# Experts' down product: both halves of the contraction as three fp32r products, and two more residual tiles parked in DRAM

## The reference

```python
def swiglu(h, w_gu, w_down):
    gate, up = jnp.split(h @ w_gu, 2, axis=-1)      # w_gu  1024 x 512
    return (jax.nn.silu(gate) * up) @ w_down        # w_down 256 x 1024

    def expert_block(acc, blk):
        tok, wts, e = blk
        out = swiglu(h_pad[tok], w_gu[e], w_down[e])
        return acc.at[tok].add(out * wts[:, None].astype(out.dtype)), None
```

## Time and profile before

| | us |
|---|---|
| median of 3 runs (2133.29 to 2133.43) | 2133.34 |
| profiled execution, its own time | 2129.38 |
| span of the profiled execution | 2127.6 |
| TensorE busy in the span | 2043.8 (96%) |
| VectorE busy | 1310.2 (62%) |
| ScalarE busy | 1008.7 (47%) |

### The profile page before, as it was taken

How to read it: one execution, slowest core, us unless ns; L and a number is a source line. 1 busy time by engine, 2 the same in 40 slices (tenths; PEclk the granted TensorE clock), 3 DMA queues, 4 the chain that set the end, 5 groups by cost and what they waited for, 6 DMA issues and landing times.

```text
span 2127.6 us, 33319 instructions
## 1 busy us (share of the span) xinstructions
PE 2043.8 (96%) x12264; PEld 1696.5 (80%) x12265; DVE 1310.2 (62%) x1968; ACT 1008.7 (47%) x1474; POOL 279.5 (13%) x217
## 2 busy tenths in 40 slices
PE   7999989999999999999999998999999999999998
PEld 3788977889767667777767767998978897898898
DVE  3868578445778668888868867357643444423433
ACT  4335455323467667777767754334332224312322
POOL 0004023000222332333333310000000000000000
PEclk9999999999999999999999999999999999999999
DMA  9831111262789879999979973211122223222221
GB/s 356 290 121 45 57 60 60 98 253 120 281 315 335 295 257 356 352 365 370 367 282 374 363 268 133 80 60 42 60 82 95 99 80 109 96 83 99 98 81 60
DMA packets 76953, 393.56 MB, mean 185 GB/s; under 512 B 16353, under 2 KB 32865, under 8 KB 46337
## 3 DMA queue, kind: packets, MB, share of 16 engines
q1 hardware_dynamic: 57794, 358.38, 44.8%
q0 software_dynamic: 19008, 33.22, 6.3%
HBM read 384.56 MB, written 43.01 MB: 201 GB/s over the span
## 4 chain that ended last, share of the span: by engine, by line
PE 61%; DMA 5%; DVE 4%; ACT 2%; issue 2%; DVEq 0%; SPq 0%; POOLq 0%; ACTq 0%
PE bank L3402 17%; PE bank L2306 4%; PE bank L2332 4%; PE bank L2310 4%; PE bank L2309 4%; DMA moe_work<-in_experts_dram 4%; PE bank L3085 3%; PE bank L3087 3%; PE bank L3086 3%; PE bank L3070 2%; PE bank L3072 2%; PE bank L3071 2%; PE bank L2292 2%; DVE moe_gu_rest L2067 1%; PE bank L2335 1%
## 5 line engine op out<-in xcount | busy, mean ns | idle before, releaser
L2687 DVE TENSOR_TENSOR b_w_rest<-ring,b_w_high 128x2048 fp32r<-128x2048 f32 x63 | 144.4, 2292 | 179.6 <-ACT b_w_high L2682 179.2
L2306 PE MATMUL bank<-moe_gu_high,moe_x_high 128*128 128x512 f32 x512 | 210.2, 411 | 17.0 <-DVE moe_gu_rest L2067 9.6
L2682 ACT ACTIVATE b_w_high<-ring 128x2048 fp32r<-128x2048 f32 x63 | 120.5, 1912 | 177.3 <-PE bank L3402 126.8
L2309 PE MATMUL bank<-moe_gu_rest,moe_x_high 128*128 128x512 f32 x512 | 202.5, 396 | 0.0
L2310 PE MATMUL bank<-moe_gu_high,moe_x_rest 128*128 128x512 f32 x512 | 202.5, 395 | 0.0
L3086 PE MATMUL bank<-b_w_rest,b_h_high 128*128 128x256 f32 x608 | 171.6, 282 | 0.0
L3085 PE MATMUL bank<-b_w_high,b_h_high 128*128 128x256 f32 x544 | 156.9, 288 | 2.8 <-DVE b_h_rest L2717 1.7
L2067 DVE TENSOR_TENSOR moe_gu_rest<-moe_work,moe_gu_high 128x2048 fp32r<-128x2048 f32 x64 | 146.3, 2286 | 18.0 <-ACT moe_gu_high L1804 17.8
L3087 PE MATMUL bank<-b_w_high,b_h_rest 128*128 128x256 f32 x544 | 153.9, 283 | 0.0
L2067 DVE TENSOR_TENSOR moe_gu_rest<-ring,moe_gu_high 128x2048 fp32r<-128x2048 f32 x64 | 146.3, 2287 | 11.1 <-ACT moe_gu_high L1804 11.1
L3402 PE MATMUL bank<-b_w_high,hidden_high 128*128 128x256 f32 x512 | 144.9, 283 | 0.0
(11 more groups left out here) (524 smaller groups left out, 5318.5 us busy)
## 6 DMA issues: line engine op xcount, KB each, us to landing
ring<-in_stream_dram SPq DMA_DIRECT2D x105, 1024.0 KB, 4.9
moe_work<-in_experts_dram SPq DMA_DIRECT2D x32, 2048.0 KB, 13.0
moe_work<-in_experts_dram SPq DMA_DIRECT2D x64, 1024.0 KB, 7.4
ring<-in_experts_dram SPq DMA_DIRECT2D x32, 2048.0 KB, 13.4
X<-in_stream_dram SPq DMA_DIRECT2D x16, 512.0 KB, 7.5
mixer_work<-in_stream_dram SPq DMA_DIRECT2D x16, 512.0 KB, 6.1
X<-in_x_dram SPq DMA_DIRECT2D x8, 512.0 KB, 8.7
ffn_sums<-mixer_work SPq DMA_DIRECT2D x8, 512.0 KB, 4.9
```

What stands on the lines that cost most here:

```text
L2306: first = mm(banks[2][:, :], xh[:, k, :], wh[h][:, c], start=(k == 0), stop=False)
L2309: mm(banks[2][:, :], xh[:, k, :], wl[h][:, c], start=False, stop=False)
L2682: nc.scalar.activation(high_at(u), raw(u), ACT.Copy).then_inc(s["w_high"], 1)
L2687: nc.vector.tensor_tensor(WL[u % FEED], raw(u), high_at(u), ALU.subtract).then_inc(s["w_rest"], 1)
```

## The change

Both halves of the down product become three fp32r products. For that ScalarE copies both halves of the down weights to `DH` (two passes of 1,024 columns per expert in place of one), VectorE subtracts twice (two passes in place of one), the transposed hidden activations are copied and subtracted as 256 columns at once (one ScalarE pass in place of two of 128), and TensorE issues six fp32r products per output half in place of one plain and three. The two more `DH` buffers lie in the tiles 1 and 2 of `X`, so these are stored to DRAM too: behind the rows of h2 of the same tile at the end of the stage before, and loaded back behind the experts. Some small buffers move. The diff, without the like edits for the further blocks:

```diff
@@ -176,7 +176,7 @@
             "xn": nc.dram_tensor("h2_rows", [TOK, D], F32),
             "rows": nc.dram_tensor("ada_rows", [1, 4 * D], F32),
             "sums": [nc.dram_tensor(f"ffn_sums{k}", [TOK, D], F32) for k in range(2)],
-            "last_rows": nc.dram_tensor("residual_last_tile", [P, D], F32),
+            "parked": nc.dram_tensor("residual_tiles", [NT * P, D], F32),
         }
 
         s_unit = [es.enter_context(nc.semaphore(f"unit_arrived{i}")) for i in range(RING)]
...
@@ -475,8 +475,10 @@
             for t in range(NT):
                 sp.wait_ge(s["h2_ready"], t + 1)
                 sp.dma_start(dram["xn"][t * P:(t + 1) * P, :], H2[:, t, :]).then_inc(s["h2_stored"], 16)
+                if t in (1, 2):
+                    sp.dma_start(dram["parked"][t * P:(t + 1) * P, :], X[:, t, :]).then_inc(s["h2_stored"], 16)
             sp.wait_ge(s["zero_stored"], 32 * NT)
-            sp.wait_ge(s["h2_stored"], 16 * NT)
+            sp.wait_ge(s["h2_stored"], 16 * (NT + 2))
 
         @block.gpsimd
         def _(pool):
...
@@ -1498,13 +1500,14 @@
     ONEHOT = [grid(mem["place"](f"onehot{k}", EXACT + 816 + 256 * k, 512, BF16)[:, :], 4) for k in range(2)]
     ONEHOTX = grid(mem["place"]("onehot_further", EXACT + 1328, 512, BF16)[:, :], 4)
     CNT = take(NE).bitcast(I32)
-    SG, HID, HDT = take(256), take(256), [take(P) for _ in range(2)]
+    SG, HID = take(256), take(256)
     HDT_AT = at[0]
-    take(256)
-    HDTH = [exact(f"hidden_high{k}", AT_WORK + HDT_AT + P * k, P) for k in range(2)]
-    HDTL = [exact(f"hidden_rest{k}", AT_WORK + WORK + P * k, P) for k in range(2)]
-    DH = [exact(f"down_high{k}", o, D) for k, o in enumerate((AT_X + (NT - 1) * D, EXACT + 1712))]
-    DL = [exact(f"down_rest{k}", AT_WORK + 2 * GU + DN * k + D, D) for k in range(2)]
+    take(512)
+    HDTH = [exact(f"hidden_high{k}", AT_WORK + HDT_AT + 256 * k, 256) for k in range(2)]
+    HDTL = [exact(f"hidden_rest{k}", AT_ADAROW + 512 + 256 * k, 256) for k in range(2)]
+    DH_AT = ((AT_X + D, AT_X + 3 * D), (AT_X + 2 * D, EXACT + 1712))
+    DH = [[exact(f"down_high{p}{k}", DH_AT[p][k], D) for k in range(2)] for p in range(2)]
+    DL = [[exact(f"down_rest{p}{k}", AT_WORK + 2 * GU + DN * p + D * k, D) for k in range(2)] for p in range(2)]
 
     TOKI, ROWI = take(4).bitcast(I32), take(4).bitcast(I32)
     TWA, TWX = take(136).rearrange("p (e c) -> p e c", c=2), [take(2) for _ in range(2)]
...
@@ -1690,12 +1693,15 @@
             sums_back(1)
             sp.wait_ge(s["dn_done"], NE - 1)
             sp.wait_ge(s["rows_moved"], 32)
-            sp.dma_start(X[:, NT - 1, :], dram["last_rows"][:, :]).then_inc(s["rows_moved"], 16)
+            sp.wait_ge(s["shared_down_in"], 16)
+            sp.dma_start(X[:, 1, :], dram["parked"][P:2 * P, :]).then_inc(s["shared_down_in"], 16)
             unit_in(0)
             sums_back(2)
             sums_back(3)
             unit_in(1)
+            sp.dma_start(X[:, 3, :], dram["parked"][3 * P:4 * P, :]).then_inc(s["rows_moved"], 16)
             sp.wait_ge(s["dn_done"], NE)
+            sp.dma_start(X[:, 2, :], dram["parked"][2 * P:3 * P, :]).then_inc(s["rows_moved"], 16)
             unit_in(2)
             unit_in(3)
             then["sync"](sp)
...
@@ -1836,15 +1842,16 @@
             def copy_hdt(i, o):
                 after(act, "ht2_done", i, o, 1)
                 after(act, "dn_done", i, o - 2, 1)
-                nc.scalar.activation(HDTH[o % 2], banks[3][:, P:2 * P], ACT.Copy).then_inc(s["down_highs"], 1)
-                nc.scalar.activation(HDT[o % 2], banks[3][:, 0:P], ACT.Copy).then_inc(s["down_highs"], 1)
+                nc.scalar.activation(HDTH[o % 2], banks[3][:, 0:2 * P], ACT.Copy).then_inc(s["down_highs"], 1)
 
             def dn_high(i, o):
                 act.wait_ge(s_dn[o % 2], 16 * (o // 2 + 1) + 32 * i)
                 after(act, "dn_done", i, o - 2, 1)
                 if isinstance(i, int) and 4 * i + o == 0:
                     act.wait_ge(s["rows_moved"], 32)
-                nc.scalar.activation(DH[o % 2], dnslot[o % 2][:, D:2 * D], ACT.Copy).then_inc(s["down_highs"], 1)
+                for k in range(2):
+                    nc.scalar.activation(DH[o % 2][k], dnslot[o % 2][:, D * k:D * (k + 1)], ACT.Copy).then_inc(
+                        s["down_highs"], 1)
 
             def further_split(n):
                 for h in range(2):
...
@@ -2069,13 +2075,15 @@
 
             def dn_rest(i, o):
 
-                after(dve, "down_highs", i, o, 1, 3)
-                v.tensor_tensor(DL[o % 2], dnslot[o % 2][:, D:2 * D], DH[o % 2], ALU.subtract).then_inc(s["down_rests"], 1)
+                for k in range(2):
+                    after(dve, "down_highs", i, o, 1 + k, 3)
+                    v.tensor_tensor(DL[o % 2][k], dnslot[o % 2][:, D * k:D * (k + 1)], DH[o % 2][k], ALU.subtract).then_inc(
+                        s["down_rests"], 1)
 
             def hdt_rest(i, o):
 
                 after(dve, "down_highs", i, o, 3, 3)
-                v.tensor_tensor(HDTL[o % 2], banks[3][:, P:2 * P], HDTH[o % 2], ALU.subtract).then_inc(s["down_rests"], 1)
+                v.tensor_tensor(HDTL[o % 2], banks[3][:, 0:2 * P], HDTH[o % 2], ALU.subtract).then_inc(s["down_rests"], 1)
 
             def x_rest(i, o):
 
...
@@ -2218,6 +2226,7 @@
             f_both(1)
             weighted(1)
             next_inverse(0)
+            dve.wait_ge(s["shared_down_in"], 32)
             mixed(1)
             sums_of_two(2)
             next_inverse(1)
...
@@ -2229,9 +2238,9 @@
             f_both(3)
             then["w_rest"](dve, 1)
             weighted(2)
+            dve.wait_ge(s["rows_moved"], 64)
             mixed(2)
             weighted(3)
-            dve.wait_ge(s["rows_moved"], 48)
             mixed(3)
             dve.wait_ge(s["f_tile"], 2 * NT)
             for t in (2, 3):
...
@@ -2313,29 +2322,26 @@
             def turn_hidden(i, o):
                 after(pe, "hid_ready", i, o, 1)
                 after(pe, "down_highs", i, o - 1, 3, 3)
-                after(pe, "down_rests", i, o - 1, 2, 2)
+                after(pe, "down_rests", i, o - 1, 3, 3)
                 for k in range(2):
                     last = nc.tensor.transpose(banks[3][:, k * P:(k + 1) * P], HID[:, k * P:(k + 1) * P], ident)
                 last.then_inc(s["ht2_done"], 1)
 
             def down_ready(i, o, bank=4):
                 after(pe, "down_highs", i, o, 3, 3)
-                after(pe, "down_rests", i, o, 2, 2)
+                after(pe, "down_rests", i, o, 3, 3)
                 if bank == 4:
                     after(pe, "out_act", i, o - 1, 2, 2)
-                pe.wait_ge(s_dn[o % 2], 16 * (o // 2 + 1) + 32 * i)
-
-            def down_products(bank, j, k, o, plain, high, rest):
-
-                c = slice(512 * j, 512 * (j + 1))
-                if k == 0:
-                    return mm(bank[:, :], plain, dnslot[o % 2][:, c], start=True, stop=False)
-                mm(bank[:, :], high, DH[o % 2][:, c], start=False, stop=False)
-                mm(bank[:, :], high, DL[o % 2][:, c], start=False, stop=False)
-                return mm(bank[:, :], rest, DH[o % 2][:, c], start=False, stop=True)
+
+            def down_products(bank, j, k, o, high, rest):
+
+                c, at = slice(512 * j, 512 * (j + 1)), slice(P * k, P * (k + 1))
+                mm(bank[:, :], high[:, at], DH[o % 2][k][:, c], start=(k == 0), stop=False)
+                mm(bank[:, :], high[:, at], DL[o % 2][k][:, c], start=False, stop=False)
+                return mm(bank[:, :], rest[:, at], DH[o % 2][k][:, c], start=False, stop=(k == 1))
 
             def down_part(i, o, j, k, bank=4):
-                product = down_products(banks[bank + j], j, k, o, HDT[o % 2], HDTH[o % 2], HDTL[o % 2])
+                product = down_products(banks[bank + j], j, k, o, HDTH[o % 2], HDTL[o % 2])
                 if (j, k) == (1, 1):
                     product.then_inc(s["dn_done"], 1)
 
...
```

24 lines of the change are left out of this document (11 added, 13 removed).

## The result

The changed kernel takes 2173.23 us (median of 4 runs, 2170.92 to 2175.27), the kernel before 2133.32 on the same chip (4 runs): a ratio of 1.0198, 95% interval 1.0185 to 1.0212. It is 2% slower. The profiled execution went from 2129.38 to 2175.27 us, its span from 2127.6 to 2173.5, +45.9; the sum of the prediction had said +41.7 between profiled executions.

A forecast was written before the change was run, and what follows sets the result against it. TensorE sets the calm pace, 9.94 us per expert; a silu-to-silu chain of 9.64 lies close, stretched to 10.78 by the pass. Ordinary experts +38.1, with special intervals and the end +41.7: 2133.34 + 41.7 = 2175, range 2163 to 2189.

The forecast's parts named there:

- The chain and its price: Silu to silu through VectorE's rests: the added pass makes ordinary experts 10.78 us each, +38.1 over 54.
- TensorE's saving is lost: Down product: 0.44 us saved per expert, spent waiting about 1.2 us before the second half.
- ScalarE's second pass costs nothing: Second dn_high copy ends 0.20 us before VectorE wants it: cost 0, at most 0.1 per expert if late.
- Late loads vanish: Down weights: ScalarE's 13.9 us of waits in 21 experts disappear as loads get more room.
- the lateness stays: Rival: down-weight loads stay as late relative to use, +13.9 on top, 2189 us; chance 0.10.
- The nine special intervals: Long silu intervals: two first-loop-pass, three second blocks, three searches, one scatter wait; +4.6 in sum.
- The two of the first loop pass: TensorE's first pass through its loop: two intervals with long waits and lower clock gain 0.44 each, -0.9.
- The searches: Three intervals searching for a second block, steps following w_rest in the chain: +1.13 each, +3.4.
- the second blocks: Three experts with a second block: pass adds 1.13, shorter down product saves 0.44; +0.7 each, +2.1.
- The end and the parking: Behind the experts -1.0, between -2 and +1; storing and reloading two more tiles 0.
- The clock rival: Waits of 1.2 us per expert lower TensorE's clock: +104 in every expert, +26 in every fourth, 2201; chance 0.07.
- The hidden pass: Rival: VectorE's extra pass costs the chain nothing, TensorE's saving counts, pace 9.64, time 2108; chance 0.05.

The follow-up runs named there:

- The single-pass experiment: Kernel before, with the parking and one more unused VectorE subtraction of 1,024 columns ahead of dn_rest: 2175.16 us, ratio 1.0215.
- the two-pass one: Kernel before, with the parking and two extra VectorE passes ahead of dn_rest, the second in all experts but the last: 2256.61 us, ratio 1.0601.
- the version without the second rest: Changed kernel without VectorE's subtraction for the down weights' second half, whose products take the first half's rest: 2123.85 us, ratio 0.9972.
- the version without the first rest: Changed kernel without VectorE's subtraction for the down weights' first half; all products take the second half's rest: 2163.84 us, ratio 1.016.
- all four versions: Changed kernel, second half's rest on GpSimd, behind or ahead of its gather, VectorE's rest in place or behind w_rest: 2175.79, 2201.48, 2314.88, 2191.78 us.
- the last version: Changed kernel, second half's rest on GpSimd ahead of its gather, VectorE's first-half rest behind the next expert's w_rest: 2191.78 us, ratio 1.0297.
- the early GpSimd pass: Changed kernel, second half's rest on GpSimd ahead of its gather, VectorE's first-half rest left in place: 2314.88 us, ratio 1.0865.
- e8: Changed kernel, second half's rest on GpSimd behind its gather, first half's on VectorE behind the next expert's w_rest: 2201.48 us, ratio 1.034.
- e1: Changed kernel with both VectorE dn_rest passes behind the next expert's w_rest, but ahead of any second block: 2148.27 us, ratio 1.008.
- e9: Kernel before with its one dn_rest moved behind the next expert's w_rest: 2129.57 us, ratio 1.0003.

## Why the prediction was right

Forecast 2175, measured 2173.2. By its steps:

- **The chain and its price.** Right. Predicted 10.78 per ordinary expert, 54 of them for +38.1; measured 584.2 us for the 54, +40.1. Of these, 51 lie between 10.71 and 10.92, 10.79 each; the rest are the first two (12.18, with a low clock, and 11.28) and one of 10.23 behind the scatter wait. The single-pass experiment shows that the pass alone makes this (584.0 us for the same 54), the two-pass one that the chain passes on each further 1.13, and the version without the second rest that the interval falls back to 9.6 where loads allow (10.04 on average).
- **TensorE's saving is lost.** Right: 12 products in some 2.85 us, and a wait of 0.96 (predicted about 1.0 as recorded).
- **ScalarE's second pass costs nothing.** Right, with 0.32 to spare where 0.20 was expected; the version without the first rest shows what it costs without that cover.
- **Late loads vanish.** Right: the wait of the earlier trace rows is gone from the larger ones, and the ordinary intervals hardly differ. So the rival "the lateness stays" (0.10) is out.
- **The nine special intervals.** Wrong in its terms, +7.1 against +4.6 in sum. The two of the first loop pass lost 6.2 us instead of 0.9: they are 11.16 and 10.82 now, since neither the long waits nor the low clock of the earlier trace rows are there; why the waits went is open. The searches gained 7.9 instead of 3.4, the second blocks 6.4 instead of 2.1. What was left out is that waits already there grow to about 2 us with the pass and can bring the low clock, at some 1.5 us each: three times in the searches, in two of the three second blocks. Without those five the searches come to +3.4 as predicted, and the second blocks to +3.4, three times the pass: the 0.44 that I credited to each for the shorter down product was not gained. The wait of 12.74 became 11.64, 1.1 less, where I had 0. The errors nearly cancel, which is luck.
- **The end and the parking.** -1.3 for everything outside the first to the last silu, against -1.0 predicted; parking 0, as measured by itself.
- **The clock rival** (0.07). It is excluded for the ordinary experts: 53 of the 54 intervals have a clock of 1.00, and the other is the stage's first, with its wait of 2.36. But it came true in five special intervals, which I had not priced. The 1.23 us at 578.12 spoke against it, and rightly for waits of that length; both low-clock intervals of the earlier trace rows hold a longer one, though, the 2.01 of the earlier trace rows and one of 2.60 at 608.03 that I had not used. That every expert has a wait does not by itself bring the fall (two extra passes, 1.7 to 1.8 us each).
- **The hidden pass** (0.05) is excluded by the experiment with one pass and nothing else.

The profiled execution says +45.9 and the medians say +39.9: the one of before lies 4 us under its median and the one of after 2 over. The prediction's own sum is between the two. That 2175 comes within 2 us of 2173 is in part luck; its ordinary part is 2 us short and its special part 2.5, this only because misses of -5.3, +4.5, +4.3 and -1.1 nearly cancel. Between profiled executions the sum was 4.2 us short; between medians it is 1.8 us over.

## What to carry to other kernels

An engine busy 79% of a stage can hold it up with each instruction, if its work lies in the chain from one step's start to the next. Measure that chain from the one place where it has already decided (here the experts with late weights), compare it with the pace, and price an added instruction by the difference. Moving work off the busiest engine gains at most the 0.3 us by which another chain lies behind it (9.94 to 9.64 in calm experts here), and over all ordinary experts it gained only 0.03 each, as down weights landed late: TensorE, the chain and the transfers were within some 4% of one another (9.94, 9.64 and 9.54 us per expert). Before a pass goes to GpSimd, ask what VectorE reads at that time.

## What the runs showed of the hardware

**GpSimd and VectorE take turns on elementwise passes over SBUF.** A GpSimd subtraction of 1,024 columns takes 2.44 to 2.74 us in the rows above when it comes first (VectorE's own 1.22). A VectorE subtraction or comparison of two SBUF operands that comes behind it ends 0.55 (`onehot`), 1.09 (`dn_rest`) or 2.15 us (`w_rest`) after GpSimd's does, its own length less 0.13; the other way round GpSimd's takes 4.15 where `w_rest` held the place. The Trainium skill states this ("SBUF — State Buffer", SBUF: two separate sides): the port pair that the two engines share is an exclusive lock, taken also by a VectorE operation with two inputs in SBUF against a GpSimd operation that reads SBUF, and whichever starts first keeps it for its whole instruction. The traces agree in all four versions, and by that rule the expectations that gave the GpSimd pass away for nothing were wrong before they ran. Offloaded so, a pass of 1.13 us costs VectorE 2.2 where it holds up `onehot` or all of `w_rest`, and in the last version 2.2 and 1.1 in turn.

**After a wait of TensorE near 2 us the clock often falls, and the length alone does not decide it.** With two extra passes, 52 waits recorded at 1.70 to 1.83 us left the clock at 2.4 GHz; the one exception is an interval of 13.43 with a wait of 1.81 at 1339.70. With the early GpSimd pass, 41 of 47 waits of 1.97 to 2.15 us were followed by some microseconds at 1.2 GHz. A fall costs 1.5 to 1.6 us, so that such a wait is nearly twice as dear as it looks. But in the version without the first rest the three waits in second blocks, 1.78 to 1.86 us, were each followed by a fall, and longer waits elsewhere were not: 2.24 with two extra passes, 2.50 at 609.49 with one, 3.25 at 799.00 with both rests moved (e8). One that was followed by a fall, and one that was not:

```profile
731.07 0.50 PE L2383 MATMUL bank<-moe_gu_high,moe_x_further_high 128*128 128x512 f32 x1 [1.86 <-DVE moe_x_further_rest L2115]
```

```profile
740.78 0.25 PE L2364 MATMUL bank<-selected,onehot_further 128*128 x4 [2.24 <-DVE onehot_further L2105]
```

No wait of 1.0 to 1.3 us in an ordinary expert of the change or of the kernel before was followed by a fall. What decides between these is open.

**A bare branch on VectorE costs 0.4 to 0.8 us.** Where the branch on the expert's count stands directly ahead of `w_rest`, with no long pass ahead of it, the profile shows 30 us of idle time that no engine ends, in 58 places with both rests behind `w_rest` (e1) and in 60 in the kernel before with its rest moved (e9). Behind `dn_rest` that gap does not appear. That the branch makes it is read from its place in the program; no run takes the branch away.
